# Fewer, larger visits to the key pages: five page groups instead of four for part of the run

## What is computed

```
past_ik = cache_idx_k[page_table].reshape(DB, PAST_LEN, IDX_DIM)        # 8 samples x 2048 keys
score = index_scores(iq, iw, concat(past_ik, ik))                       # 8 index heads, relu, weighted sum
_, idx = lax.top_k(where(causal, score, -inf), topk)                    # topk = 256 of 2052
k_sel = cache_k[phys, off] or the new keys; v_sel likewise              # pages of 128 keys, 4 KV heads x 128
s = einsum('bqgrd,bqkgd->bqgrk', q, k_sel) * Dh ** -0.5
o = einsum('bqgrk,bqkgd->bqgrd', softmax(s), v_sel)
```

## Time and profile before

| | |
|---|---|
| median of 3 runs | 1316.29 us |
| the profiled execution | 1313.9 us, span 1312.3 us |
| TensorE busy | 1288.4 us (98% of the span) |
| VectorE busy | 788.5 us (60%) |
| ACT busy | 599.0 us (46%) |
| granted TensorE clock, mean | 0.996 |
| DMA | 271.39 MB, 207 GB/s over the span |

### The profile page before, as it was taken

How to read it: one execution, slowest core, us unless ns; L and a number is a source line. 1 busy time by engine, 2 the same in 40 slices (tenths; PEclk the granted TensorE clock), 3 DMA queues, 4 the chain that set the end, 5 groups by cost and what they waited for, 6 DMA issues and landing times.

```text
span 1312.3 us, 25350 instructions
## 1 busy us (share of the span) xinstructions
PE 1288.4 (98%) x9660; PEld 1208.5 (92%) x9660; DVE 788.5 (60%) x1302; ACT 599.0 (46%) x977; POOL 193.5 (15%) x307
## 2 busy tenths in 40 slices
PE   9999999999999999999999999999999999999995
PEld 8988777776779999999999999999999999999995
DVE  5657877774447898755665565566556445443434
ACT  4444332344435576645654554465455333333433
POOL 4520000013310220100010010001000500120203
PEclk9999999999999999999999999999999999999998
DMA  8868899989976455555565555555555655555552
GB/s 269 238 192 318 295 366 375 284 316 386 394 268 216 139 165 172 149 175 167 154 175 165 166 154 176 163 159 167 171 163 160 201 161 161 163 162 167 166 163 72
DMA packets 101020, 271.39 MB, mean 207 GB/s; under 512 B 13369, under 2 KB 23938, under 8 KB 100770
## 3 DMA queue, kind: packets, MB, share of 16 engines
q1 hardware_dynamic: 85010, 221.74, 54.7%
q10 hardware_dynamic: 8464, 28.88, 6.5%
q0 software_dynamic: 7424, 19.15, 4.0%
HBM read 264.54 MB, written 5.18 MB: 206 GB/s over the span
## 4 chain that ended last, share of the span: by engine, by line
PE 90%; DMA 3%; DVE 2%; ACT 2%; SPq 2%; issue 1%; ACTq 0%; DVEq 0%
PE G L529 27%; PE G L530 27%; PE G L531 27%; PE A L883 2%; PE A L703 2%; DMA k_ring<-in_kT_cache 1%; DMA v_ring_x<-in_v_cache 1%; DMA raw<-in_w_iq 1%; ACT w_hi L1183 1%; DVE w_lo L1622 1%; DMA x_raw<-in_xT 1%; SPq L344 1%; PE A L803 1%; PE A L719 0%; PE A L833 0%
## 5 line engine op out<-in xcount | busy, mean ns | idle before, releaser
L1622 DVE TENSOR_TENSOR w_lo<-raw,w_hi 128x1024 fp32r<-128x1024 f32 (+1 forms) x352 | 433.0, 1230 | 386.4 <-ACT w_hi L1183 385.4
L1183 ACT ACTIVATE w_hi<-raw 128x1024 fp32r<-128x1024 f32 (+1 forms) x352 | 371.5, 1056 | 490.2 <-PE G L531 442.5
L529 PE MATMUL G<-x_hi,w_hi 128*128 128x290 f32 (+1 forms) x1664 | 500.1, 301 | 2.9 <-DVE w_lo L1622 1.8
L530 PE MATMUL G<-x_lo,w_hi 128*128 128x290 f32 (+1 forms) x1664 | 494.4, 297 | 0.0
L531 PE MATMUL G<-x_hi,w_lo 128*128 128x290 f32 (+1 forms) x1664 | 491.4, 295 | 0.0
L529 PEld LDWEIGHTS G<-x_hi,w_hi 128*128 128x128 f32 x1664 | 312.6, 188 | 11.7 <-issue 10.5
L530 PEld LDWEIGHTS G<-x_lo,w_hi 128*128 128x128 f32 x1664 | 314.1, 189 | 0.2
L531 PEld LDWEIGHTS G<-x_hi,w_lo 128*128 128x128 f32 x1664 | 312.2, 188 | 0.0
L530 PE MATMUL G<-h_lo,w_hi 128*128 128x288 f32 x704 | 209.9, 298 | 0.0
L531 PE MATMUL G<-h_hi,w_lo 128*128 128x288 f32 x704 | 209.4, 297 | 0.0
L529 PE MATMUL G<-h_hi,w_hi 128*128 128x288 f32 x704 | 208.2, 296 | 0.0
(11 more groups left out here) (345 smaller groups left out, 1363.3 us busy)
## 6 DMA issues: line engine op xcount, KB each, us to landing
raw<-in_w_up SPq DMA_DIRECT2D x176, 512.0 KB, 3.6
raw<-in_w_down SPq DMA_DIRECT2D x88, 512.0 KB, 3.6
k_ring<-in_kT_cache SPq DMA_DIRECT2D x128, 256.0 KB, 4.9
raw<-in_w_in ACTq DMA_DIRECT2D x48, 512.0 KB, 5.3
raw<-in_w_out SPq DMA_DIRECT2D x32, 512.0 KB, 6.8
v_ring_x<-in_v_cache SPq DMA_DIRECT2D x32, 256.0 KB, 5.9
v_ring_x<-in_v_cache POOLq DMA_DIRECT2D x28, 256.0 KB, 6.4
v_ring_p<-in_v_cache SPq DMA_DIRECT2D x20, 256.0 KB, 6.0
```

The lines of the kernel that those rows point to most:

```text
L529: pe.matmul(out, hi, xh, start=start, stop=False)
L530: pe.matmul(out, hi, xl, start=False, stop=False)
L1183: act.activation(w_hi[:, c, 0:width], raw[:, c, 0:width], ACT.Copy).then_inc(hi_done, 1)
L1622: dve.tensor_tensor(w_lo[:, c, 0:width], raw[:, c, 0:width], w_hi[:, c, 0:width].bitcast(f32), ALU.subtract).then_inc(lo_done, 1)
```

## The change

`units_after(i)` reads a table, `KEYS_AT`, of how many units are scored behind each chunk. Thirteen visits score two units and six score one: 19 visits in place of 26. Behind chunks 3, 5, 7, 8, 11, 13, 16 and 19 there is none. For units 4 to 19 the ring has a fifth group, `k_more`, in region r3: it takes units 4, 9, 14 and 19. `key_before(u)` and `key_next(u)` give the unit before and behind in the same group; a unit is loaded when the one before it in its group is scored. VectorE waits before `windows(0)` until 20 units are scored, since `pooled` lies in the same space.

Behind each chunk the units are, before: 3, 4, 5, 6: one each (0 to 3); 8: 4; 9: 5, 6; 10: 7; 11: 8; 12: 9, 10; 13: 11; 14: 12; 15: 13, 14; 16: 15; 17: 16; 18: 17, 18; 19: 19; 20: 20; 21: 21, 22; 22: 23; 23: 24; 24: 25; 25: 26, 27; 26: 28; 27: 29; 28: 30; 29: 31. Now: 4: 0, 1; 6: 2, 3; 9: 4, 5; 10: 6, 7; 12: 8, 9; 14: 10, 11; 15: 12, 13; 17: 14, 15; 18: 16, 17; 20: 18, 19; 21: 20, 21; 22: 22; 23: 23; 24: 24; 25: 25, 26; 26: 27; 27: 28, 29; 28: 30; 29: 31.

```diff
--- before.py
+++ after.py
@@ -104,13 +104,38 @@
     return NPG * (4 * (step // 4) + b) + 4 * (step % 4) + i
 
 
+KEYS_AT = {4: 2, 6: 2, 9: 2, 10: 2, 12: 2, 14: 2, 15: 2, 17: 2, 18: 2, 20: 2, 21: 2, 22: 1, 23: 1, 24: 1, 25: 2, 26: 1,
+           27: 2, 28: 1, 29: 1}
+FIVE = range(4, 20)
+
+
 def units_after(i):
 
-    twice = (9, 12, 15, 18, 21, 25)
-    if i < 3 or i == 7 or i > 29:
-        return range(0)
-    first = i - 3 - (i > 7) + sum(d < i for d in twice)
-    return range(first, first + 1 + (i in twice))
+    first = sum(n for at, n in KEYS_AT.items() if at < i)
+    return range(first, first + KEYS_AT.get(i, 0))
+
+
+def key_group(u):
+
+    if u in FIVE:
+        return (4, 0, 1, 2, 3)[(u - 4) % 5]
+    return u % 4
+
+
+def key_turns(u):
+
+    return sum(key_group(w) == key_group(u) for w in range(u + 1))
+
+
+def key_before(u):
+
+    before = [w for w in range(u) if key_group(w) == key_group(u)]
+    return before[-1] if before else None
+
+
+def key_next(u):
+
+    return [w for w in range(u + 1, 32) if key_before(w) == u]
 
 
 def layer(nc, xT, w_iq, w_ik, w_in, w_out, w_up, w_down, kT_cache, v_cache, ik_cache, pages,
@@ -187,6 +212,7 @@
     ik_a = put("ik_a", [128, DB, 4, PAGE], f32, r3)
     pooled = put("pooled", [128, 8, T], f32, r3)
     wp_sb = put("wp_sb", [128, 4, 2, 256], f32, r3 + 8 * T * 4)
+    k_more = put("k_more", [128, UNIT, 512], f32, r3)
     a_hi = put("a_hi", [128, 8, T], f32r, r3)
     a_lo = put("a_lo", [128, 8, T], f32r, r3 + 8 * T * 4)
     r4 = region(8 * P_EXT * 4)
@@ -260,7 +286,7 @@
         x_in = [sem(f"x_in{c}") for c in range(8)]
         consts_in, late_in, pages_in = sem("consts_in"), sem("late_in"), sem("pages_in")
         ik_in = [sem("ik_in_a"), sem("ik_in_b"), sem("ik_in_b2")]
-        k_in = [sem(f"k_in{r}") for r in range(KR // UNIT)]
+        k_in = [sem(f"k_in{r}") for r in range(KR // UNIT + 1)]
         v_first = [sem("v_first0"), sem("v_first1")]
         v_even = [sem(f"v_even{r}") for r in range(VR // UNIT + 1)]
         v_odd = [sem(f"v_odd{r}") for r in range(VR // UNIT + 1)]
@@ -329,6 +355,10 @@
                 eng.dma_start(ik_b[64 * j:64 * j + 64, b, i, :],
                               ik_cache[bass.ds(r, 1)].rearrange("a p n -> p (a n)")).then_inc(ik_in[1], 16)
 
+        def key_slot(u, i):
+
+            return k_more[:, i, :] if key_group(u) == 4 else k_ring[:, UNIT * key_group(u) + i, :]
+
         def load_key_unit(eng, kind, u):
 
             if u == 0:
@@ -338,11 +368,13 @@
                 eng.wait_ge(wsel_kept, 2)
                 eng.wait_ge(iq_roped, 4)
                 eng.wait_ge(ik_roped, 1)
-            if u >= 4:
-                eng.wait_ge(k_used, u - 3)
+            if u == 4:
+                eng.wait_ge(s_raw, 4)
+            if key_before(u) is not None:
+                eng.wait_ge(k_used, key_before(u) + 1)
             for i, r in enumerate(page_numbers(kind, key_page(UNIT * u))):
-                eng.dma_start(k_ring[:, UNIT * (u % 4) + i, :],
-                              kT_cache[bass.ds(r, 1)].rearrange("a p n -> p (a n)")).then_inc(k_in[u % 4], 16)
+                eng.dma_start(key_slot(u, i),
+                              kT_cache[bass.ds(r, 1)].rearrange("a p n -> p (a n)")).then_inc(k_in[key_group(u)], 16)
 
         def value_group(u):
 
@@ -453,9 +485,11 @@
                     sp.dma_start(wp_sb[:], w_pool).then_inc(late_in, 16)
                 if i < 3:
                     load_key_unit(sp, SPE, i + 1)
+                if i == 3:
+                    load_key_unit(sp, SPE, 4)
                 for u in units_after(i - 1):
-                    if u + 4 < 32:
-                        load_key_unit(sp, SPE, u + 4)
+                    for w in key_next(u):
+                        load_key_unit(sp, SPE, w)
                 if i == 25:
                     sp.wait_ge(g_free, 4 * (SL_P + 2))
                     sp.dma_start(pT_out, p_ext[:, :, P_OUT:P_EXT]).then_inc(p_out, 16)
@@ -689,7 +723,8 @@
             def sample_scores(w):
 
                 step, u = w // 4, w % 4
-                b, slot = 4 * (step // 4) + u, UNIT * w % KR
+                b, slot = 4 * (step // 4) + u, UNIT * key_group(w)
+                pages = k_more[:] if key_group(w) == 4 else k_ring[:, slot:slot + UNIT, :]
                 bank = step % 2
                 if w == 0:
                     pe.wait_ge(q_padded, DB + 1)
@@ -698,10 +733,10 @@
                     pe.wait_ge(p_relu, IH)
                 if step >= 2 and u == 0:
                     pe.wait_ge(qk_kept, step - 1)
-                pe.wait_ge(k_in[w % 4], 16 * UNIT * (w // 4 + 1))
+                pe.wait_ge(k_in[key_group(w)], 16 * UNIT * key_turns(w))
                 for h in range(KVH):
                     mm = pe.matmul(A[32 * h:32 * h + 32, bank, :], q_pad[:, b, 2 * h:2 * h + 2, :],
-                                   k_ring[:, slot:slot + UNIT, 128 * h:128 * h + 128],
+                                   pages[:, :, 128 * h:128 * h + 128],
                                    start=u == 0, stop=u == 3)
                 mm.then_inc(k_used, 1)
 
@@ -1904,6 +1939,7 @@
                     dve.wait_ge(k_roped, KVH)
                     dve.wait_ge(late_in, 96)
                 if i == 21:
+                    dve.wait_ge(k_used, 20)
                     windows(0)
                     windows(1)
                 if i == 22:
```

## The result

The changed kernel took 1323.99 us (median of 6 runs, 1320.04 to 1325.12) against 1313.96 us of the kernel before on the same chip (6 runs, 1310.3 to 1318.78): ratio 1.0075, 95% interval 1.0059 to 1.009. It is slower by 10.0 us. The profiled execution took 1320.04 us, the shortest of the six; its span is 1318.4 us. The mean granted clock was 0.992 or 0.993 in each of the six executions, and 0.996 in the profile of the kernel before.

A forecast was written before the change was run, and what follows sets the result against it. TensorE's own stream was taken as the bound (busy 1288.4 of 1312.3 us). The terms 1.64 - 0.72 + 0.86 + 0.86 + 3.7 gave +6.3 us, on the median 1316.3 a forecast of 1322.6, range 1315 to 1327.5.

The forecast's parts named there:

- no difference: Whole kernel: a time within about 0.5% of the kernel before (1309.7 to 1322.9 us), chance 0.55.
- Chunks 3 to 7, +1.64: Pairs in chunks 4 and 6 delay VectorE's chain; M8, middle `total` matmul of chunk 8, comes 1.64 us later.
- A bare chunk is bounded by VectorE: Without a visit, E (matmul behind the chunk's last) waits for VectorE's count: M (middle `total`) + 1.50, not 1.0.
- M behind a bare chunk with `rope_key`: Chunks 12 and 14: `rope_key` keeps VectorE busy, so the next middle `total` matmul is 0.47 us late.
- Chunks 8 to 20, -0.72: M8 to M20, middle `total` matmuls of those chunks: 0.72 us shorter, counting page waits and M20's wait as gone.
- a steady 0.9 us: TensorE's waits for key pages in the kernel before, 0.9 us in all, taken as gone after the change.
- Unit 29 waits for its pages, +3.7: Chunk 27: unit 29's pages queue behind the `pT_out` store, so TensorE waits 3.7 us (0 to 5).
- Rival (d), the lower clock: Chunk 27: the 3.7 us wait lowers TensorE's clock to 1.2 GHz; +9.6 us, 1326, chance 0.07.
- (a): Chunk 27: unit 29's pages come in time, no wait; +2.6 us, 1318.9, chance 0.29.
- (b): Bare chunks: VectorE keeps up and fewer visits simply pay; -1.8 us, 1314.5, chance 0.06.
- (c): From chunk 12 on: second units' pages need over 15 us, three or four more waits; 1328, chance 0.14.
- M + 1.0: Bare chunks: E 1.0 us behind the middle `total` matmul, no VectorE wait; named as a sign the forecast is wrong.

The follow-up runs named there:

- experiment 4: The changed kernel with units 0 to 3 scored one by one behind chunks 3 to 6 again: 1320.87 us, ratio 1.0062 to the kernel before.
- experiments 5 and 6: VectorE's 31 counting passes over 272 of 544 columns: in the changed kernel 1321.46 us (ratio 1.0055), in the kernel before 1312.13 us (0.9985).
- Experiments 1 and 2: First: changed kernel, store of `pT_out` in chunk 27 instead of 25, 1315.79 us. Second: kernel before, units 29 and 30 both behind chunk 27, 1317.16 us.
- experiment 3: The changed kernel with 20 unused matmuls of ones ahead of unit 29, filling its page wait: 1320.63 us, ratio 1.0058 to the kernel before.
- `early_single`: Same run as experiment 4: the changed kernel with units 0 to 3 scored singly behind chunks 3 to 6, 1320.87 us.
- experiment 7: The changed kernel with units 0 to 3 single behind chunks 3 to 6 and the `pT_out` store in chunk 27: 1314.12 us, ratio 0.9999.
- `before_again`: The kernel before, unchanged, profiled once more: one time of 1314.61 us.
- `before_late`: The kernel before with only the store of `pT_out` issued in chunk 27 instead of 25: 1311.73 us, ratio 0.9984.
- `rope_pairs`: The changed kernel's five groups with 26 visits, pairs only behind chunks 9, 11, 13, 15, 18 and 25: 1312.46 us, ratio 0.999 to the kernel before.
- `filled_wait`: Same run as experiment 3: the changed kernel with 20 unused matmuls ahead of unit 29, 1320.63 us.

## Why the prediction was right, and where its size was off

The forecast was +6.3 us (1322.6), and +10.0 was measured (1323.99), inside the range; the change is slower, which had 0.41, not the likelier "no difference". That 1322.6 is only 1.4 off is in part luck: it was added to 1316.29, the median of three executions, and with three more that median is 1313.96, from which +6.3 gives 1320.3. The size of the change was 3.7 us too small.

- *Chunks 3 to 7, +1.64*: right. +1.71, each M within 0.08 of its worked value, and experiment 4 takes it away with the pairs.
- *A bare chunk is bounded by VectorE*: right. M + 1.50, 2.02 and 2.29 as worked out, and experiments 5 and 6 shift them with VectorE's counts alone. M behind a bare chunk with `rope_key` is 0.45 late, where I had 0.47.
- *Chunks 8 to 20, -0.72*: the working for the changed kernel was right (62.61 worked out, 62.79 and 62.76 measured), the one for the kernel before was not. I took its late pages as a steady 0.9 us. They delayed the totals by 1.28, and the second profile of before has none; against it the stretch is 0.74 slower (62.76 to 62.02). This mis-sized term is up to 1.5 us in one execution; with late pages in four profiles of five, the forecast stands nearer to the usual one.
- *Unit 29 waits for its pages, +3.7*: right in place and cause, 4.37 and 5.05 in size. Unit 29's last page took 10.8 us, the slowest of the earlier trace rows 10.2. Experiments 1 and 2 show the cause from both sides: the store ahead in SyncE's queue, and a chunk that wants the unit which stands behind it.
- *Rival (d), the lower clock*: it came, on top of the forecast, with a chance given of 0.07. This is the step that failed: I set the wait and the clock apart as rivals though the second follows from the first. It costs 1.8 us (experiment 3) to 2.5 (13.07 - 5.48 - 5.05 in the second profile, 5.48 being 4.62 + 0.86; 1.7 in `early_single`, where V27 to V28 is 11.53) and not the 3.3 that I had worked out, since part of the slow stretch fell on the wait and the clock was back within the next chunk. By the Trainium skill (TensorE: Matmul & The Clock Gate, "Why this matters for your kernels") an idle gap of this length between bursts halves the clock; the trace agrees (0.50 in 250 to 254), and by that rule the forecast would have been (d)'s 1326, or 1324.6 with the 2 us that it really costs.
- *Rivals (a), (b), (c)* are out: V27 to V28 waits in each profile; E never came at M + 1.0; and no other unit waited in the profile of the changed kernel, so the 14.5 to 16 us that units 13, 15, 17 and 21 had were enough.

The sum from M4 to V28 by the traces is 1.71 - 0.54 + 0.78 + 7.40 = 9.35 between the first profiles and 1.70 + 0.74 + 0.77 + 7.39 = 10.6 between the second; the medians say 10.0. But behind V28 the changed kernel is 0.9 and 2.9 us shorter, where 0 was forecast: there the kernel before waited 0.71 and 1.84 us for the value page near 376, and the changed kernel had no such wait (0.73 at 387 in its second profile). So what the profiles show to the end is 8.5 and 7.8, and the 1.5 to 2 us more of the medians are open. The clock is no chance of the profiles: its mean is below 0.994 in all seven executions of the changed kernel, and 0.994 or more in 43 of the 45 executions of the kernel before in the sets of experiments 1 to 4 and 5 to 8.

## What to carry to other kernels

Fewer visits to a side job did not pay by themselves (experiment 7): a chunk left bare waits for the other engine. What paid was to move single units to the chunks in which the partner is late anyway, with as many visits as before. Ask of every moved transfer what stands ahead of it in its queue; in the changed kernel a store of short rows there cost more than all regrouping of visits. And a wait of several microseconds on TensorE is to be priced with the lower clock behind it, as one term.

## What the runs showed of the hardware

- A page wait of 4.0 to 6.4 us at unit 29 or 30 was followed by a granted clock of 0.50 in each of the five profiles that have one, for one to three windows of 2 us behind it. Shorter waits went either way. The kernel before itself has one such place, a value page near 376. In `before_again` TensorE waited 1.84 us there and the clock was 0.50 behind it, which with the longer wait is most of the 2.2 us by which the last stretch of the second profile in the table is longer; in `before_late` it waited 1.73 at the same place and the clock stayed at 1.00 throughout. A wait of 1.92 for a value page at 376 (`rope_pairs`) was followed by 0.50 until past 385, and one of 2.02 (`early_single`, at 383) by 1.00 throughout. From that wait's end to TensorE's turning of `o_mix` (line 993) the two take 12.98 and 8.67 us: the wait of 1.9 us cost 4.3 more. The waits of 1.08, 1.27 and 1.39 at V28 cost no clock, but 1.38 and 0.23 us close together, at 305 in `filled_wait`, were followed by 0.50 in 308 to 310. So whether a wait of 1.4 to 2 us lowers the clock can't be told from its length. TensorE's timeline and a window of `before_again`:

```profile
375.98 1.93 PE L883 MATMUL A<-v_ring_x,p_tok 128*32 128x512 f32 x8 [1.84 <-DMA v_ring_x<-in_v_cache]
```

```profile
376.00:378.00 2.00, 2.00 (x9) 0.34 (x9) 0.00 (x0) 0.00 (x0) 0.00 (x0) 0.50 1.04 409
```

- A page of 256 KB issued in 239 to 240.8 lands in 3.8 to 4.3 us, and in 10.8 with the store of 668-byte rows (167 numbers) ahead of it in the same queue. In 236 to 244 the store's kernel moves 221 GB/s, the other 306.
- The first 33 us of the program differ between profiles: M4 stands at 120.22 and 118.94 in the two of the kernel before, at 117.86 and 118.09 in those of the changed one. Waits for pages of 0.2 to 1.4 us come and go. A single profile's "just in time" is not a bound.
